# Second mixer: the attention half's output norm ahead of the S5 half's, and S5 tiles interleaved with attention units four to seven

## The chip, the cores and the metric

The kernel runs on one core of a Trainium2 chip. Five engines work side by side and meet only through semaphores: TensorE (PE in the profile; PEld is its weight load), VectorE (DVE), ScalarE (ACT), GpSimd (POOL) and SyncE (SP), which issues most of the transfers. The metric is the time of one execution in device microseconds, as the median of several runs. All times below are of that kind.

## What is computed

Two transformer blocks over 512 tokens of width 1024, in float32. The change lies in the second block's mixer. It projects the normed input to `u`, `q`, `k`, `v`; an S5 state-space layer runs on `u` (a linear recurrence over the tokens, then `gelu`, then a gate), and attention with a sliding window of 128 tokens and a sink runs on `q`, `k`, `v`. Each half gets its own RMS norm, and both together go through `w_out`:

```python
    _, _, s_re, s_im = lax.associative_scan(combine, (a_re_t, a_im_t, bu_re, bu_im), axis=1)
    y = (jnp.einsum("blgp,ghp->blgh", s_re, c_re) - jnp.einsum("blgp,ghp->blgh", s_im, c_im)
         + d_skip.reshape(N_SSM_GROUPS, SSM_GROUP) * ug)
    z = jax.nn.gelu(y.reshape(bsz, seq, D_SSM))
    y_ssm = z * jax.nn.sigmoid(z @ w_glu + b_glu)
...
    m = jnp.maximum(jnp.max(logits, axis=-1, keepdims=True), sink)
    p = jnp.exp(logits - m)
    probs = p / (jnp.sum(p, axis=-1, keepdims=True) + jnp.exp(sink - m))
    y_attn = jnp.einsum("bnhgqk,bnkhd->bnqhgd", probs, v_band)
...
    mixed = jnp.concatenate([_rms(y_ssm, out_norm_ssm), _rms(y_attn, out_norm_attn)], axis=-1)
    x = x + g1 * (mixed @ w_out)
```

After it comes the second block's feed-forward layer.

## The kernel before

Every engine has one hand-written list of instructions. No scheduler changes it: what stands first is issued first, and an instruction whose semaphore has not come holds all that is behind it on its engine. So the order of work in the second mixer is the order of the calls at the end of each engine's part.

**Number format.** A float32 product is made of three passes on PE: a tensor is split in `hi` (a rounded copy, made by ACT) and `lo` (the rest, made by DVE), and `hi*hi`, `hi*lo` and `lo*hi` are summed in a PSUM bank. Weights come in panels of 1 MB: SP loads a panel in `w_raw`, `split(n)` on ACT makes `w_hi`, `split(n)` on DVE makes `w_lo`. There are two buffers of each. The sums of squares, the transposes, scores and values work in plain float32.

**The eight PSUM banks** `B[0]` to `B[7]` are handed out by hand. Banks 0 to 3 are for attention units (even ones use 0 and 1, odd ones 2 and 3), bank 7 takes a unit's values, and the small functions `u2_bank`, `u_bank`, `input_bank`, `chunk_bank`, `turned_bank`, `glu_bank`, `out2_bank` say which bank a piece of S5 or of the output uses. Bank 5 takes the sum of squares of the S5 norm (`ps`), bank 7 that of the attention norm (`pa`).

**The attention** has eight units (four blocks of 128 queries, two key heads). One unit goes PE `sw_scores`, DVE `sw_max` (bias, row maximum), ACT `sw_exp` (four exponentials with their sums), DVE `sw_scale`, PE `sw_turn` (transposes), ACT `sw_turned` (copy to `pT`), PE `sw_values`, ACT `sw_out` (copy from bank 7 to `yat`). The next unit's `sw_values` waits for it, since bank 7 is the only one.

**S5** goes PE `project` (pieces of `u2_products`, 96 matmuls in all), ACT `u2_moved`, PE `chunk_turn`, ACT `u_moved`, PE `chunk_inputs`, DVE `chunks` (two halves, each a scan over 64 chunks), PE `within_chunks` and `from_states`, ACT `chunk_out`, PE `turn_back`, ACT `s5_gelu` (the gelu, then `z_hi`), DVE `z_split` (`z_lo`), PE `glu` (four tiles of 12 matmuls), ACT `gates`, DVE the product `ys`.

**The norms.** For `ps` and `pa` alike ACT makes four squares, PE sums them with four matmuls against `ones` (`norm`), ACT takes the inverse root (`norm_root`), DVE improves it in three steps, and then for each of four tiles DVE makes `h`, ACT `h_hi`, DVE `h_lo`. The squares of `ps` go through two slots of `tmp`, so the third and fourth wait for PE. Then PE multiplies with `w_out`: the first two panels tile by tile of the sum (`by_k`), S5 half (`ks` 0 to 3) first and the attention half after it, the last two panels as `features`. The norm `p2` and the feed-forward loops follow.

**ACT's function tables.** When ACT goes from one kind of function to another (exponential, gelu, sigmoid, inverse root), the compiler puts an `ACT_TABLE_LOAD` ahead.

SP's list waits for the last `project` matmul, then loads two tables for S5 and the first panels of `w_out`. The functions and lines that the steps below touch stand in the printed code.

Of the kernel before, what the change touches and what calls it, by code (L numbers as in the profile page):

```python
# [25 lines left out]
F32 = mybir.dt.float32  # L26
# [105 lines left out]
def build(nc, inp, rel_onehot, out):  # L132
# [12 lines left out]
    with ExitStack() as ctx:  # L145
# [53 lines left out]
        def overlay(size, *tiles):  # L199
# [55 lines left out]
         z_hi, z_lo, yat_sq) = overlay(  # L255
# [4 lines left out]
            (12, "wb", [P, NS, 2, 2, P // 2], F32), (16, "gate", [P, 4, T], F32),  # L260
# [4 lines left out]
            (12, "z_hi", [P, 4, T], F32R), (24, "z_lo", [P, 4, T], F32R), (4, "yat_sq", [P, 4, T], F32),  # L265
# [18 lines left out]
        def u_bank(q):  # L284

            return B[(5, 6, 4, 5)[q]]
# [5 lines left out]
        def chunk_bank(q):  # L292

            return B[(4, 7, 4, 7)[q]]

        def turned_bank(q):

            return B[(5, 6, 4, 5)[q]]

        def glu_bank(t):  # L300

            return B[(6, 4, 5, 6)[t]]

        def out2_bank(t):

            return B[(4, 6, 5, 0, 1, 2, 3, 4)[t]]
# [25 lines left out]
        NORM_PARTS = {"n1": (KD, KD), "nm": (KD, 2), "n2": (KD, 2), "p1": (KD, 2), "ps": (4, 4), "pa": (4, 4), "p2": (KD, 2)}  # L332
# [3 lines left out]
        for name in NORMS:  # L336
            before = [NORM_PARTS[b] for b in NORMS[:len(NORM)]]
            NORM[name] = sum(tiles for tiles, _ in before)
            NORM_SQ[name] = sum(NORM_PARTS[b][1] for b in NORMS[:len(NORM) - 1] if b != "pa")
# [304 lines left out]
        def _(act):  # L644
# [32 lines left out]
            def norm_cast(name, hi=h_hi, shift=None):  # L677

                for k in range(NORM_PARTS[name][0]):
# [348 lines left out]

            u2_moved(0)
            u2_moved(1)  # L1030
            sw_exp(0)
            u2_moved(2)
            sw_exp(1)
            sw_turned(0)
            sw_turned(1)
            sw_out(0)
            u2_moved(3)
            sw_out(1)
            u_moved(0)
            sw_exp(2)  # L1040
            for q in (1, 2, 3):
                u_moved(q)
            sw_exp(3)
            split(PART["glu"][0])
            sw_turned(2)
            sw_turned(3)
            sw_out(2)
            sw_out(3)
            chunk_out(0)
            chunk_out(1)  # L1050
            act.wait_ge(S("scan_out"), 4)
            s5_gelu((0, 1))
# [3 lines left out]
            sw_exp(4)  # L1056
            sw_exp(5)
            sw_turned(4)
            sw_turned(5)
            gates((0, 1))  # L1060
            sw_out(4)
            gates((2, 3))
            split(PART["glu"][0] + 1)
            sw_out(5)
            sw_exp(6)
            norm_squares("ps", ys, lambda eng, k: eng.wait_ge(S("glu_out"), k + 1))
            sw_exp(7)
            split(PART["glu"][0] + 2)
            norm_root("ps", T)
            sw_turned(6)  # L1070
            sw_turned(7)
            sw_out(6)
            sw_out(7)
            act.wait_ge(S("sw_out"), 2 * len(SW_UNITS))
            for k in range(4):
                act.activation(yat_sq[:, k, :], yat[:, k, :], ACT.Square).then_inc(S("yat_squared"), 1)
            norm_cast("ps", h_hi[:, 0:4])
            norm_root("pa", T)
            norm_cast("pa", h_hi[:, 4:8])
            n = PART["w_out2"][0]  # L1080
# [28 lines left out]
        def _(dve):  # L1109
# [15 lines left out]
            def norm(name, tiles, gain, shift=None, hi=None, lo=None, width=D, panel=None):  # L1125
# [9 lines left out]
                for k in range(count + 1):  # L1135
                    if k < count:
# [591 lines left out]
            chunks(0)  # L1728
            chunks(1)
            sw_max(4)  # L1730
            sw_max(5)
            split(PART["glu"][0])
            z_split(range(4))
            sw_scale(4)
            sw_scale(5)
            sw_max(6)
            sw_max(7)
            for t in range(4):
                dve.wait_ge(S("glu_gate"), t + 1)
                dve.tensor_tensor(ys[:, t, :], ys[:, t, :], gate[:, t, :], ALU.mult).then_inc(S("glu_out"), 1)  # L1740
            split(PART["glu"][0] + 1)
            sw_scale(6)
            sw_scale(7)
# [685 lines left out]
```

## Time and profile before

| | us |
|---|---|
| median of 3 runs | 1877.11 |
| lowest and highest | 1875.33, 1881.25 |
| the profiled execution's own time | 1880.06 |
| its span, first to last instruction | 1878.6 |
| PE busy | 1824.4 (97%) |
| DVE, ACT, POOL busy | 1027.0, 722.5, 168.9 |
| mean granted TensorE clock | 0.984 |

The span of the profiled execution is 1878.6 us, 1.5 less than its time; its time is 2.95 above the median. The profile counts from the first instruction. The second mixer's own stretch, from the first `project` matmul to the first matmul of the norm `p2`, is 1314.5 to 1490.2 us. A row of the timeline gives the start, the length, the engine, the line, and in brackets how long the engine had been idle before it and who ended that. Rows that follow each other without a gap are merged (x8 is eight instructions). A plain float32 matmul shows as two.

### The profile page before, as it was taken

The page shows a single profiled execution, that of the slowest core. Times are in us where ns is not written, and L with a number is a line of the kernel's source. Part 1 is how long each engine was busy: PE and PEld are TensorE (multiplying, and loading weights), DVE is VectorE, ACT ScalarE, POOL GpSimd, SP SyncE. Part 2 cuts the span into 40 slices and gives each one's busy share as a digit, 9 for nine tenths or more (in the row PEclk, how much of TensorE's full clock was granted, in tenths as well). Part 3 has the DMA queues.
Part 4 walks back from the last instruction along what each step waited for, and adds up shares of the span by engine and source line. Part 5 has one row for each costly group of instructions (what it writes and reads, how often), then busy time and mean ns, then how long its engine had stood idle before and what let it go on. Part 6 is the DMA issues. An engine that isn't in the chain of part 4 may idle for free.

```text
span 1878.6 us, 23478 instructions
## 1 busy us (share of the span) xinstructions
PE 1824.4 (97%) x8801; PEld 1450.6 (77%) x8801; DVE 1027.0 (55%) x1433; ACT 722.5 (38%) x1015; POOL 168.9 (9%) x232
## 2 busy tenths in 40 slices
PE   7999999999999999999999999998997999999998
PEld 5888888868887777876887788887974688888887
DVE  5655436464564556555788733436485455555433
ACT  4222222333434787422332222224545245555322
POOL 2222001110000000005111110100000300000000
PEclk9999999999999999999999999999998999999999
DMA  6766422233222112223654552234211223322222
GB/s 205 236 213 214 144 70 92 93 120 102 90 82 80 63 46 68 68 90 97 206 167 135 152 151 79 90 106 174 109 34 45 67 90 101 100 89 78 89 87 81
DMA packets 171691, 206.77 MB, mean 110 GB/s; under 512 B 18404, under 2 KB 150114, under 8 KB 171106
## 3 DMA queue, kind: packets, MB, share of 16 engines
q1 hardware_dynamic: 144994, 161.97, 26.4%
q0 software_dynamic: 12640, 38.55, 6.6%
q10 hardware_dynamic: 13984, 5.27, 1.2%
q8 instruction: 47, 0.77, 0.2%
q14 instruction: 26, 0.21, 0.0%
HBM read 190.29 MB, written 17.56 MB: 111 GB/s over the span
## 4 chain that ended last, share of the span: by engine, by line
PE 94%; DVE 3%; ACT 2%; issue 1%; DMA 0%; ACTq 0%; DVEq 0%
PE bank L1854 42%; PE bank L1818 35%; PE bank L2069 6%; PE bank L1786 2%; PE bank L1976 1%; PE bank L2093 1%; PE bank L2166 1%; PE bank L1833 1%; PE bank L1874 1%; PE bank L2104 0%; ACT prob L994 0%; PE bank L1905 0%; PE bank L2205 0%; PE bank L2095 0%; DVE scan_t L1657 0%
## 5 line engine op out<-in xcount | busy, mean ns | idle before, releaser
L659 ACT CAST w_hi<-w_raw 128x2048 fp32r<-128x2048 f32 x158 | 301.1, 1906 | 833.6 <-PE bank L1854 454.3
L1123 DVE TENSOR_TENSOR w_lo<-w_raw,w_hi 128x2048 fp32r<-128x2048 f32 x157 | 370.6, 2360 | 455.5 <-ACT w_hi L659 455.2
L1854 PE MATMUL bank<-h_hi,w_hi 128*128 128x512 f32 x1088 | 435.5, 400 | 13.4 <-ACT h_hi L683 8.9
L1854 PE MATMUL bank<-h_hi,w_lo 128*128 128x512 f32 x1088 | 433.2, 398 | 0.0
L1854 PE MATMUL bank<-h_lo,w_hi 128*128 128x512 f32 x1088 | 344.1, 398 | 0.0
L1854 PEld LDWEIGHTS bank<-h_hi,w_hi 128*128 128x128 f32 x1088 | 206.4, 190 | 65.9 <-issue 16.8
L1854 PEld LDWEIGHTS bank<-h_lo,w_hi 128*128 128x128 f32 x1088 | 206.0, 189 | 50.0
L1854 PEld LDWEIGHTS bank<-h_hi,w_lo 128*128 128x128 f32 x1088 | 206.4, 190 | 49.3 <-issue 0.2
L1818 PE MATMUL bank<-hid_hi,w_lo 128*128 128x512 f32 x528 | 208.8, 396 | 0.0
L1818 PE MATMUL bank<-hid_hi,w_hi 128*128 128x512 f32 x528 | 208.8, 396 | 0.0
L1818 PE MATMUL bank<-hid_lo,w_hi 128*128 128x512 f32 x528 | 208.8, 396 | 0.0
L1818 PEld LDWEIGHTS bank<-hid_hi,w_hi 128*128 128x128 f32 x528 | 99.2, 188 | 24.1
L1818 PEld LDWEIGHTS bank<-hid_lo,w_hi 128*128 128x128 f32 x528 | 99.2, 188 | 23.9
L1818 PEld LDWEIGHTS bank<-hid_hi,w_lo 128*128 128x128 f32 x528 | 99.2, 188 | 23.9
L589 POOL TENSOR_TENSOR tmp<-x 128x512 f32<-128x512 f32 x24 | 28.8, 1201 | 922.2 <-DVE x L1624 441.6
L1818 PE MATMUL bank<-w_hi,h_hi 128*128 128x512 f32 (+1 forms) x256 | 97.8, 382 | 0.0
L1818 PE MATMUL bank<-w_lo,h_hi 128*128 128x512 f32 (+1 forms) x256 | 97.4, 380 | 0.0
L1818 PE MATMUL bank<-w_hi,h_lo 128*128 128x512 f32 (+1 forms) x256 | 97.4, 380 | 0.0
L1272 DVE SCALAR_TENSOR_TENSOR mod_acc<-mod_raw,small,mod_acc 128x512 f32<-128x512 f32 x84 | 63.2, 752 | 28.7 <-DMA mod_raw<-in_w_mod 24.9
L1304 DVE TENSOR_TENSOR tmp<-tmp,bank 128x512 f32<-128x512 f32 x44 | 28.3, 684 | 91.7 <-PE bank L1854 91.7
L558 POOL DMA_DIRECT2D mod_raw<-in_w_mod x96 | 52.7, 549 | 191.3 <-DVE mod_acc L1269 147.4
L1766 DVE SCALAR_TENSOR_TENSOR tmp<-bank,vec,tmp 128x511 f32<-128x511 f32 x88 | 63.8, 746 | 6.5 <-DVE tmp L1766 1.7
(410 smaller groups left out, 2402.6 us busy)
## 6 DMA issues: line engine op xcount, KB each, us to landing
w_raw<-in_w_in SPq DMA_DIRECT2D x29, 1024.0 KB, 5.2
mod_raw<-in_w_mod POOLq DMA_DIRECT2D x96, 256.0 KB, 3.8
w_raw<-in_ffn_w_gate SPq DMA_DIRECT2D x22, 1024.0 KB, 7.0
w_raw<-in_ffn_w_up SPq DMA_DIRECT2D x22, 1024.0 KB, 5.5
w_raw<-in_w_up SPq DMA_DIRECT2D x22, 1024.0 KB, 5.1
w_raw<-in_ffn_w_down SPq DMA_DIRECT2D x16, 768.0 KB, 4.2
w_raw<-in_ffn_w_down SPq DMA_DIRECT2D x16, 640.0 KB, 3.9
w_raw<-in_w_out SPq DMA_DIRECT2D x8, 1024.0 KB, 5.0
```

What stands on the lines that cost most here:

```text
L558: pool.dma_start(mod_raw[:, k % MOD_SLOTS, :], wm[:, k, bass.ds(i * T + first * T, T)])\
L589: done(pool.tensor_tensor(tmp[:, min(k, 1), :], x[:, k, :], x[:, k, :], ALU.mult))
L659: act.copy(w_hi[i % 2][:], w_raw[i % 2][:]).then_inc(S("w_hi_done"), 1)
L1123: dve.tensor_tensor(w_lo[s][:], w_raw[s][:], w_hi[s][:].bitcast(F32), ALU.subtract).then_inc(S("w_split"), 1)
L1272: ins = dve.scalar_tensor_tensor(mod_acc[:], mod_raw[:, k % MOD_SLOTS, :], small[:, k:k + 1], mod_acc[:], ALU.mult, ALU.add)
L1304: dve.tensor_tensor(tmp[:, 2 + t, :], tmp[:, t, :], B[2 + t][:], ALU.mult).then_inc(S("hid"), 1)
L1766: dve.scalar_tensor_tensor(y[:, back:], up[:, :T - back], col_at(f"conv_w_2:{2 - back}", i * 2, KF * half + t), y[:, back:], ALU.mult, ALU ...
L1786: mm = pe.matmul(out_ap, stationary, moving, start=first and i == 0, stop=last and i == len(terms) - 1)
L1818: mm = pe.matmul(out_ap, stationary, moving, start=first and i == 0, stop=last and i == total - 1)
L1833: pe.matmul(sum_bank(name)[:], ones[:], square, start=direct == tiles and d == 0, stop=d == direct - 1).then_inc(S("norm_summed"), 1)
L1854: mm = pe.matmul(bank[:], w[:, k, at], h[:, k, :], start=k == first and part == 0 and i == 0, stop=k == last and part == 1)
L2069: mm = pe.matmul(beside_bank(name, t)[:], stationary, moving, start=j == 0, stop=j == 3 * k - 1)
```

## The change

Nothing is computed differently. It moves work and renames places.

- **Attention norm first.** `pa` is made before `ps` on ACT, DVE and PE. PE multiplies panel 0 with the attention half (`out2(0, "pa", ...)`), then sums the squares for `ps`, then panel 1 with the attention half, then panels 0 and 1 with the S5 half. `split(glu + 2)` on DVE comes between the two norms.
- **Squares of the S5 half** go to a tile of their own, `ys_sq`, made by ACT in one go behind `norm_cast("pa")`, and not through `tmp`.
- **Units and S5 pieces in another order.** On ACT the exponentials of unit zero stand ahead of the first `u2_moved`; units four and five run among `u_moved`, `chunk_out` and the gelu tiles; the exponentials of units six and seven stand ahead of the gates. On DVE units four and five are scaled between the two halves of `chunks`, and units six and seven ahead of the split of the first `w_out` panel. On PE `project` is cut 12, 24, 6, 26, 6, 6, 16 where it was 24, 12, 12, 30, 6, 6, 6; the scores of six and seven, and the values of four and five, stand ahead of the last `from_states`; two `glu` tiles stand ahead of the transposes of units six and seven, and the last one behind the values of both.
- **Banks and places** follow: the tables of banks, the waits at `chunk_turn`, `chunk_inputs`, `sw_values`, `within_chunks`, `turn_back`, and the overlay of the shared area (`scan_t`, `ys`, `gate`, `z_hi` move).

```diff
-            (0, "u2t", [P, NS, 2, TB, SG], F32), (0, "scan_t", [P, 4, NS // 2, NC], F32), (0, "ys", [P, 4, T], F32),
+            (0, "u2t", [P, NS, 2, TB, SG], F32), (12, "scan_t", [P, 4, NS // 2, NC], F32), (16, "ys", [P, 4, T], F32),
...
-            return B[(5, 6, 4, 5)[q]]
+            return B[(5, 6, 5, 5)[q]]
...
-            return B[(4, 6, 5, 0, 1, 2, 3, 4)[t]]
+            return B[(0, 1, 2, 3, 4, 6, 5, 0)[t]]
...
             norm_root("pa", T)
             norm_cast("pa", h_hi[:, 4:8])
+            for k in range(4):
+                act.wait_ge(S("glu_out"), k + 1)
+                act.activation(ys_sq[:, k, :], ys[:, k, :], ACT.Square).then_inc(S("ys_squared"), 1)
+            split(PART["glu"][0] + 2)
+            norm_root("ps", T)
+            norm_cast("ps", h_hi[:, 0:4])
...
-                if q == 3:
-                    pe.wait_ge(S("u_moved"), 1)
+                if q >= 2:
+                    pe.wait_ge(S("u_moved"), (1, 3)[q - 2])
...
-                pe.wait_ge(S("u_moved"), 3 + half)
+                pe.wait_ge(S("u_moved"), 2 + 2 * half)
...
                 if u == 4:
-                    pe.wait_ge(S("o_out"), 4)
+                    pe.wait_ge(S("o_out"), 2)
...
-            for part, ks in enumerate(((0, 1, 2, 3), (4, 5, 6, 7))):
-                for i in range(2):
-                    pe.wait_ge(S("w_split"), n + i + 1)
-                    by_k(n + i, [out2_bank(2 * i), out2_bank(2 * i + 1)], h_hi, h_lo,
-                         lambda k: pe.wait_ge(S("norm_split"), NORM["pa"] + k - 3 if k >= 4 else NORM["ps"] + k + 1), ks)
+
+            def out2(i, name, ks):
+
+                pe.wait_ge(S("w_split"), n + i + 1)
+                by_k(n + i, [out2_bank(2 * i), out2_bank(2 * i + 1)], h_hi, h_lo,
+                     lambda k: pe.wait_ge(S("norm_split"), NORM[name] + k % 4 + 1), ks, first=4, last=3)
+
+            out2(0, "pa", (4, 5, 6, 7))
+            norm("ps")
+            out2(1, "pa", (4, 5, 6, 7))
+            out2(0, "ps", (0, 1, 2, 3))
+            out2(1, "ps", (0, 1, 2, 3))
```

ACT of the kernel before, from the copies of units four and five (`pT`) over the gates to the two inverse roots:

```order
L1003 COPY pT<-bank 128x512 x4
L1027 ACT_TABLE_LOAD
L1027 ACTIVATE gate<-bank,vec 128x512 x2
L1011 COPY yat<-bank 64x2x128 x2
L1027 ACTIVATE gate<-bank,vec 128x512 x2
L659 CAST w_hi<-w_raw 128x2048
L1011 COPY yat<-bank 64x2x128 x2
L994 ACT_TABLE_LOAD
L994 ACTIVATE prob,stat<-prob,stat 128x256 x4
L995 ACTIVATE stat<-stat 128x4
L670 ACTIVATE tmp<-ys 128x512 x4
```

Ahead of the exponentials of unit six stand four gates, a panel split and unit five's copy; the squares of `ps` come next, and unit seven's exponentials behind them.

ACT of the changed kernel, from the last two gelu tiles (`ys`, `z_hi`) to the attention norm's squares:

```order
L1021 CAST z_hi<-ys 128x512 x2
L994 ACT_TABLE_LOAD
L994 ACTIVATE prob,stat<-prob,stat 128x256 x4
L995 ACTIVATE stat<-stat 128x4
L994 ACTIVATE prob,stat<-prob,stat 128x256 x4
L995 ACTIVATE stat<-stat 128x4
L1027 ACT_TABLE_LOAD
L1027 ACTIVATE gate<-bank,vec 128x512 x2
L1003 COPY pT<-bank 128x512 x4
L1027 ACTIVATE gate<-bank,vec 128x512
L1011 COPY yat<-bank 64x2x128 x4
L1027 ACTIVATE gate<-bank,vec 128x512
```

Both units' exponentials now stand right behind the gelu tiles and ahead of every gate, with no panel split among them.

PE of the kernel before, from the sum of squares of `ps` in bank 5 to the first matmul with `w_out`:

```order
L1833 MATMUL bank5<-tmp,ones 128x512 x4
L2244 MATMUL bank0<-ident,prob 128x128 x4
L2244 MATMUL bank1<-ident,prob 128x128 x4
L2244 MATMUL bank2<-ident,prob 128x128 x4
L2244 MATMUL bank3<-ident,prob 128x128 x4
L1786 MATMUL bank7<-pT,v2 128x512 x4
L1833 MATMUL bank7<-yat_sq,ones 128x512 x4
```

The sum of `ps` stands ahead of units six and seven, and their transposes and values ahead of the sum of `pa`.

PE of the changed kernel, the end of `out2(0, "pa")` and the start of `out2(1, "pa")`:

```order
L1869 MATMUL bank0<-h_lo,w_hi0 128x512
L1869 MATMUL bank1<-h_lo,w_hi0 128x512
L1848 MATMUL bank5<-ys_sq,ones 128x512 x4
L1869 MATMUL bank2<-h_hi,w_hi1 128x512
L1869 MATMUL bank2<-h_hi,w_lo1 128x512
```

The sum of `ps` now stands between 24 matmuls of panel 0 and 24 of panel 1. The sum of `pa` stands directly ahead of the first of these 48.

## Rows read from the trace of the kernel before

**Rows 1.** The page, part 1: busy time, share of the span, instructions.
```profile
PE 1824.4 (97%) x8801; PEld 1450.6 (77%) x8801; DVE 1027.0 (55%) x1433; ACT 722.5 (38%) x1015; POOL 168.9 (9%) x232
```
**Rows 2.** Waits of PE, 1318 to 1475: in total, times, longest.
```profile
PE bank L1833 <- ACT tmp L670: 5.5, 1, 5.5
PE bank L1818 <- DVE z_lo L1721: 3.7, 1, 3.7
PE bank L1786 <- ACT pT L1003: 2.0, 1, 2.0
PE bank L2244 <- DVE prob L1716: 1.7, 2, 1.0
PE bank L1833 <- ACT yat_sq L1076: 1.5, 1, 1.5
PE bank L1786 <- ACT yat L1011: 0.9, 1, 0.9
PE bank L2295 <- ACT oc L985: 0.5, 1, 0.5
```
**Rows 3.** Stretches of PE: length, busy, granted clock, DMA share, GB/s.
```profile
1392.70:1399.50 6.80, 5.04 (x12) 0.50 0.47 157
...
1420.00:1426.80 6.80, 5.41 (x7) 0.50 0.45 154
...
1433.70:1440.50 6.80, 5.75 (x7) 0.50 0.40 139
```
**Rows 4.** Timeline of PE: start, us, line, what.
```profile
1349.26 7.36 PE L2205 MATMUL bank<-ident,u2t 128*128 128x64 f32 x64
...
1394.46 0.77 PE L1818 MATMUL bank<-z_hi,w_hi 128*128 128x512 f32 x1 [3.67 <-DVE z_lo L1721]
...
1399.64 1.03 PE L2244 MATMUL bank<-ident,prob 128*128 128x128 f32 x8
...
1421.39 6.38 PE L1833 MATMUL bank<-tmp,ones 128*128 128x512 f32 x8 [5.51 <-ACT tmp L670]
1427.61 1.04 PE L2244 MATMUL bank<-ident,prob 128*128 128x128 f32 x8
...
1441.90 3.70 PE L1833 MATMUL bank<-yat_sq,ones 128*128 128x512 f32 x8 [1.51 <-ACT yat_sq L1076]
1445.04 0.79 PE L1854 MATMUL bank<-h_hi,w_hi 128*128 128x512 f32 x1
```
**Rows 5.** Timeline of ACT: last copy of `u2t`, last gate, table load, squares.
```profile
1348.56 0.65 ACT L974 COPY u2t<-bank 128x256 f32<-128x256 f32 x2 [3.46 <-PE bank L2166]
...
1414.21 0.69 ACT L1027 ACTIVATE gate<-bank,vec 128x512 f32<-128x512 f32 x1 [1.32 <-PE bank L1818]
...
1417.36 1.28 ACT L994 ACT_TABLE_LOAD   x1
...
1441.22 2.19 ACT L1076 ACTIVATE yat_sq<-yat 128x512 f32<-128x512 f32 x4
```
**Rows 6.** Timeline of DVE and ACT: panel split, last gelu tiles.
```profile
1389.66 2.29 DVE L1123 TENSOR_TENSOR w_lo<-w_raw,w_hi 128x2048 fp32r<-128x2048 f32 x1
...
1391.75 1.14 ACT L1021 CAST z_hi<-ys 128x512 fp32r<-128x512 f32 x2
1391.87 2.49 DVE L1721 TENSOR_TENSOR z_lo<-ys,z_hi 128x512 fp32r<-128x512 f32 x4
```
**Rows 7.** Timeline of ACT and DVE: the norm `pa`.
```profile
1447.25 0.69 ACT L675 ACTIVATE rstd<-bank,small 128x512 f32<-128x512 f32 x1
...
1451.59 0.69 DVE L1147 TENSOR_TENSOR h_lo<-tmp,h_hi 128x512 fp32r<-128x512 f32 x1
...
1452.86 0.69 DVE L1147 TENSOR_TENSOR h_lo<-tmp,h_hi 128x512 fp32r<-128x512 f32 x1
```
**Rows 8.** Stretches: length, PE, PEld, DVE, ACT, POOL busy, granted clock.
```profile
1390.00:1445.00 55.00, 40.35 (x155) 23.37 (x151) 28.16 (x42) 35.83 (x77) 0.00 (x0) 0.81 0.17 58
1445.00:1467.50 22.50, 22.50 (x97) 17.99 (x96) 14.59 (x19) 6.33 (x8) 4.31 (x3) 1.00 0.00 1
```

More of the change, by code:

```diff
@@ L338, in build @@
             NORM[name] = sum(tiles for tiles, _ in before)
-            NORM_SQ[name] = sum(NORM_PARTS[b][1] for b in NORMS[:len(NORM) - 1] if b != "pa")
+            NORM_SQ[name] = sum(NORM_PARTS[b][1] for b in NORMS[:len(NORM) - 1] if b not in ("pa", "ps"))
             NORM_SUM[name] = sum(direct + (direct < tiles) for tiles, direct in before)
@@ L1047, in _ @@
             sw_out(2)
+            sw_exp(4)
+            sw_exp(5)
+            u_moved(2)
             sw_out(3)
+            u_moved(3)
+            split(PART["glu"][0])
+            split(PART["glu"][0] + 1)
             chunk_out(0)
             chunk_out(1)
-            act.wait_ge(S("scan_out"), 4)
-            s5_gelu((0, 1))
+            sw_turned(4)
+            sw_turned(5)
+            s5_gelu((0, ))
+            sw_out(4)
+            s5_gelu((1, ))
+            sw_out(5)
             chunk_out(2)
@@ L1055, in _ @@
             s5_gelu((2, 3))
[L1056 to L1059, printed above, removed]
+            sw_exp(6)
+            sw_exp(7)
             gates((0, 1))
[L1061 to L1069, printed above, removed]
             sw_turned(6)
             sw_turned(7)
+            gates((2,))
             sw_out(6)
             sw_out(7)
+            gates((3,))
             act.wait_ge(S("sw_out"), 2 * len(SW_UNITS))
@@ L1123, in split, with norm @@
                 dve.tensor_tensor(w_lo[s][:], w_raw[s][:], w_hi[s][:].bitcast(F32), ALU.subtract).then_inc(S("w_split"), 1)
-            def norm(name, tiles, gain, shift=None, hi=None, lo=None, width=D, panel=None):
+            def norm(name, tiles, gain, shift=None, hi=None, lo=None, width=D, panel=None, between={}):
                 hi, lo = (h_hi, h_lo) if hi is None else (hi, lo)
@@ L1727, in _, with gated @@
                 sw_scale(u + 1)
[L1728 to L1729 removed]
             sw_max(4)
             sw_max(5)
+            chunks(0)
+            sw_scale(4)
+            sw_scale(5)
+            chunks(1)
+            sw_max(6)
+            sw_max(7)
             split(PART["glu"][0])
             z_split(range(4))
[L1734 to L1738, printed above, removed]
+            sw_scale(6)
+            sw_scale(7)
+            split(PART["glu"][0] + 1)
+            def gated(t):
                 dve.wait_ge(S("glu_gate"), t + 1)
                 dve.tensor_tensor(ys[:, t, :], ys[:, t, :], gate[:, t, :], ALU.mult).then_inc(S("glu_out"), 1)
[L1741 to L1743 removed]
+            for t in range(4):
+                gated(t)
+            norm("pa", yat, lambda k: col("out_norm_attn_2", k), hi=h_hi[:, 4:8], lo=h_lo[:, 4:8], width=T)
             split(PART["glu"][0] + 2)
             norm("ps", ys, lambda k: col("out_norm_ssm_2", k), hi=h_hi[:, 0:4], lo=h_lo[:, 0:4], width=T)
[L1746 removed]
             n, panels, _ = PART["w_out2"]
@@ L2325, in _ @@
             sw_scores(3)
-            project(6)
             sw_values(1)
-            for q in range(4):
-                chunk_turn(q)
-            chunk_inputs(0)
+            project(16)
+            chunk_turn(0)
+            chunk_turn(1)
             sw_turn(2)
@@ L2334, in _ @@
             sw_values(2)
+            sw_scores(5)
+            chunk_inputs(0)
+            chunk_turn(2)
+            sw_values(3)
+            chunk_turn(3)
+            within_chunks(0)
             chunk_inputs(1)
-            sw_scores(5)
-            sw_values(3)
-            within_chunks(0)
             within_chunks(1)
@@ L2341, in _ @@
             from_states(1)
+            sw_turn(4)
+            sw_turn(5)
             within_chunks(2)
```

77 lines of the change are left out of this document (39 added, 38 removed).

## The prediction

> **What bounds the kernel now.** I read the page first. PE is busy 97% of the span and no other engine more than 55% [rows 1], so time can only be won where PE stands still or runs slowly. The change leaves every matmul as it is; it decides what PE finds in front of it. So I went to PE's waits inside the second mixer, then to the granted clock of its stretches, then to the timelines of PE, ACT and DVE around each wait.
>
> The waits [rows 2] add up to 5.5 + 3.7 + 2.0 + 1.7 + 1.5 + 0.9 + 0.5 = 15.8 us. The reader should see who is named: the squares of the S5 norm, the split of the gelu tiles, the copies and probabilities of units six and seven, the squares of the attention norm.
>
> The clock is the second loss. Three times the granted clock is 0.50, that is 1.2 GHz and not 2.4, for 6.8 us, each time after or amid waits: it fell 1.9 us into the wait for `z_lo`, late in the wait for the first square of `ps`, and behind the short waits of units six and seven. In these stretches PE was busy for 5.04 + 5.41 + 5.75 = 16.2 us [rows 3]. At half the clock half of that is lost: 8.1 us. A second way to count agrees. The first `glu` tile took 1399.64 - 1394.46 = 5.2 us for 12 matmuls, 0.43 each, where 96 at the full clock fill the 22.5 us of the next stretch, 0.234 each [rows 4, 8]; and the four sums for `ps` took 1427.61 - 1421.39 = 6.2 us against 1445.04 - 1441.90 = 3.1 for `pa` [rows 4]. (That one holds short waits for squares beside the clock.)
>
> Together 15.8 + 8.1 = **23.9 us are lost** in the second mixer before, nearly all of it from 1390 to 1445. That is the pot from which the change can win.
>
> [...] In 1390 to 1445 PE is busy for 40.35 of 55 us, PEld for only 23.37, where a stretch without a gap has PEld at 17.99 of 22.50, or 80% [rows 8]. [...]
>
> **The change part by part.** I carried the new order forward: each engine takes its list in turn, each step starts when its engine is free and its semaphore has come, with the lengths of the rows. What PE still waits for is this.
>
> *Start, to the end of `project`.* The first exponentials no longer stand behind copies of `u2t`, and 26 matmuls cover them: the first wait for `prob` (0.7 of the 1.7 in [rows 2]) goes. But the last 16 `project` matmuls now stand directly ahead of `chunk_turn`, which needs their copy. Before, the values of unit one lay between and hid it: the copy starts at 1348.56 and PE goes on at 1349.26 [rows 4, 5]. Bare, it costs the length of those values, **1.0 us**.
>
> *Units four and five among the scans.* Here each wait has a cover, and I name the thin ones. `chunk_turn(3)` waits for the third `uc`, which ACT copies behind the exponentials of units four and five: 1.0 us to spare. `chunk_inputs(1)` waits for the fourth `uc`, behind unit three's copy: 0.9. `from_states(0)` waits for the first scan, behind four row maxima: 1.3. The values of unit five wait for bank 7: **0.2 us**. The second scan on DVE starts 4 us later, behind the scaling of units four and five, but `from_states(2)` stands later too and has 4 to spare. SP's list is the same and its table loads still follow `project`, with over 10 us to spare. The panel split on ACT ahead of `chunk_out(0)` falls in time in which ACT waits for PE anyway.
>
> *The wait for `z_lo`.* Before, DVE was busy with a panel split until 1391.87, so all four tiles of `z_lo` came at the end (2.49 us), though `z_hi` was ready earlier [rows 6]. Now two tiles are done long before, and the chain is ACT's alone: last `z_hi` at 1392.9, one `z_lo` of 0.7, so PE starts 0.7 us earlier. 3.7 becomes **3.0**; the 0.5 wait for `oc` goes, as the `turn_back` steps are spread out.
>
> *Units six and seven.* The 5.5 us wait was ACT's list: from the last gate at 1414.21 a panel split, unit five's copy, a table load at 1417.36, the exponentials, and only then a square [rows 5]. All of this now lies ahead of the gates, under 24 `glu` matmuls. So do the exponentials of unit seven (1.0 of `prob`) and the copies of `pT` that stood behind the S5 root (2.0). Gone: 5.5 + 1.0 + 2.0. Bank 7 still holds the values of unit seven back: **0.9**, as before.
>
> *The squares for `pa`.* PE ends `glu(3)`, ACT must make the last gate (0.69) and the first square (0.6 of 2.19 for four) before PE can sum [rows 5]; with the hand-overs **1.6 us**, where it was 1.5.
>
> *The chain of `pa` is now bare.* This is the price. Before, the sums for `pa` were followed by the S5 half of `w_out`. Now nothing stands between them and `out2(0, "pa")`. From the root to the first `h_lo` the chain took 1451.59 + 0.69 - 1447.25 = 5.03 us [rows 7]; with the end of the sums ahead and PE's start behind, **5.4 us**. No table load adds to it: it runs while PE sums.
>
> *The chain of `ps` is covered, barely.* The sums for `ps` follow `out2(0, "pa")`, and 24 matmuls of panel 1 stand behind: 24 x 0.234 = 5.6 us of cover for a chain of 5.3 to 5.4. After that DVE delivers a tile each 1452.86 - 1451.59 = 1.27 us [rows 7], and PE needs 6 x 0.234 = 1.4. I take nought, with 0 to 0.5 as bounds. The last two panels are as they were.
>
> *Idle after:* 1.0 + 0.2 + 3.0 + 0.9 + 1.6 + 5.4 = 12.1 us, against 15.8. **Gain 3.7.**
>
> *Clock after.* The trace of before doesn't show the new order's clock, so I go by its two like waits. A wait of 3.7 brought a spell of 6.8 us that began 1.9 us in; a wait of 5.5 brought one that began 4.1 us in, since PE stopped at about 1415.9 [rows 3, 4]. If the waits of 3.0 and 5.4 do the same, 6.8 - 1.1 = 5.7 and 6.8 - 1.3 = 5.5 us of work fall in them: 11.2 against 16.2, and half of the difference is **2.5 us gained**. The third spell had waits of 1.0 and 2.0 us ahead of it, and the new order has 0.9 and 1.6 there; I take it as gone. The bounds are one spell fewer (2.8 us more gained) and one more (3.4 less).
>
> The sum is 3.7 + 2.5 = 6.2 us. Against the profiled execution that makes 1880.06 - 6.2 = 1873.9; that execution is 2.95 above the median, and I put the gain on the median: 1877.11 - 6.2 = **1870.9 us**. What is uncertain in the hand-overs (some 0.1 us for each of a dozen) makes 1 us to either side.
>
> **The rivals.**
>
> *A third spell.* Waits of 0.9 and 1.6 us stay around the values of unit seven, with only `glu(3)` between, and before waits of 1.0 and 2.0 were enough. For it: they lie close. Against: they are shorter and hold 2.8 us of full work between them. Price: 6.8 us of work at half the clock, 3.4. Time: 1870.9 + 3.4 = 1874.3. This would be no change.
>
> *A thin cover tears.* If the S5 chain takes over 5.6 us, or the third `uc` is over 1.0 us late, PE waits for the rest, one to one, and what hangs on it moves too. For it: covers of 0.2 to 1.3 us at five places. Against: my rows include the hand-overs at most of them. Price 1 to 3: 1873 on the middle.
>
> *One spell less.* If the wait for `z_lo` is so short that the clock holds, 2.8 more are won: 1868.1. For it: the chain has the least in front of it of all. Against: 3.0 is not far from 3.7, and waits of 2.0 and less had a spell behind them.
>
> *Slower: the clock stays down.* From the first `glu` tile to the end of the 96 `w_out` matmuls PE has 45 us of work, broken by waits of 0.9, 1.6 and 5.4. If each recovery is cut off by the next wait, the half clock holds on. Each 6.8 us spell more costs 3.4, so two more eat the whole gain and from four more it is slower than 1882.7, the bound of what can be measured: 1870.9 + 4 x 3.4 = 1884.5. Against: before, the clock was back at 1.00 after each of three spells though the waits went on, and the 22.5 us behind them ran at 1.00 [rows 3, 8].
>
> *It doesn't do what it says.* The lists are fixed, so the order does change; but the waits could only move, the bare chain of `pa` (5.4) taking the place of the one removed (5.5). It gives 1877 if all other gains fail as well. Against: the waits of 2.0, 1.0, 0.7 and 0.5 go for reasons of their own.
>
> **How the numbers follow.** A difference of 0.3%, 5.6 us, is about what a measurement of this kernel can tell from none. The forecast, 1870.9 with a range of its own from 1869 to 1873, has 0.50. The third spell has 0.18, a torn cover 0.12, one spell less 0.10, nothing gained 0.05, slower 0.05. Faster by over 5.6 us means below 1871.5: three quarters of the forecast (0.38), one spell less (0.10) and a little of the torn covers (0.02), 0.50. Slower by over 5.6 us has 0.05. The rest, 0.45, is within 0.3%. The range of 8 in 10 runs from 1867 to 1876: below it lies half of the one-spell-less case, above it the slower one and nothing gained.
>
> **What would show it.** Right: PE has no wait for an S5 square and none for `pT`; one wait of 5.2 to 5.6 at the first `w_out` matmul; 2.6 to 3.3 ahead of `glu(0)`; 1.0 ahead of `chunk_turn(0)`; none at the first matmul of `out2(1, "pa")`; PE's waits in the mixer sum to 12; two stretches with the granted clock at 0.50, not three. Wrong: waits for `uc` or for the scans, a second wait of some us at panel 1, or a third stretch at 0.50 between `glu(0)` and `w_out`. The rest of the kernel, up to 1314 us and from the norm `p2` on, should take as long as before.

## The result, and the profile after

The changed kernel takes 1871.3 us in the median of 8 runs (1870.9 to 1875.5). The kernel before took 1880.4 in the median of 8 (1875.1 to 1881.3): the three runs shown ahead and five beside the changed kernel, four of which lie above 1880. The ratio is 0.9964, 95% interval 0.9953 to 0.9976: 0.36% faster, some 6.8 us. The medians lie 9.1 us apart and the means 6.9 (1879.0 and 1872.1), so the ratio is the safer figure. The same kernel run again with the experiments gave 0.9965 (0.9951 to 0.9978). The profiled execution took 1870.98 us, its span is 1869.5.

The page, part 1, of the changed kernel; it answers to [rows 1]:

```profile
PE 1819.3 (97%) x8801; PEld 1450.8 (78%) x8801; DVE 1026.7 (55%) x1433; ACT 721.8 (39%) x1014; POOL 168.9 (9%) x232
```

PE is busy 5.1 us less and the span is 9.1 shorter, so the share reads 97% as before. PE's waits in the second mixer, the view of [rows 2] (us in total, times, longest):

```profile
PE bank L1869 <- DVE h_lo L1153: 5.2, 1, 5.2
PE bank L1829 <- DVE z_lo L1727: 3.0, 1, 3.0
PE bank L1848 <- ACT yat_sq L1075: 1.3, 1, 1.3
PE bank L1797 <- ACT yat L1011: 0.9, 1, 0.9
PE bank L2220 <- ACT u2t L974: 0.7, 1, 0.7
```

Five waits, 11.1 us, where seven made 15.8. The S5 squares, the copies of `pT`, the probabilities and `oc` are no longer waited for. The two stretches at half clock, as [rows 3] shows three (columns: length, busy of PE, PEld, DVE, ACT, POOL, then granted clock, DMA share, GB/s):

```profile
1397.97:1404.80 6.83, 5.85 (x14) 4.62 (x15) 3.56 (x8) 6.78 (x21) 0.00 (x0) 0.50 0.22 75
1428.69:1435.52 6.83, 5.92 (x14) 4.75 (x15) 3.95 (x7) 5.39 (x9) 0.00 (x0) 0.50 0.01 2
```

Between them the clock is 1.00, that is 2.4 GHz. PE's timeline at the places that the prediction named, first and last row marking the mixer's stretch (it answers to [rows 4]):

```profile
1312.94 0.51 PE L2181 MATMUL bank<-w_hi,h_hi 128*128 128x512 f32 x1
...
1347.39 3.79 PE L2220 MATMUL bank<-ident,u2t 128*128 128x64 f32 x32 [0.74 <-ACT u2t L974]
...
1398.95 0.77 PE L1829 MATMUL bank<-z_hi,w_hi 128*128 128x512 f32 x1 [3.00 <-DVE z_lo L1727]
...
1429.60 0.77 PE L1869 MATMUL bank<-h_hi,w_hi 128*128 128x512 f32 x1 [5.21 <-DVE h_lo L1153]
1430.16 0.63 PE L1869 MATMUL bank<-h_hi,w_lo 128*128 128x512 f32 x1
1430.58 0.63 PE L1869 MATMUL bank<-h_hi,w_hi 128*128 128x512 f32 x1
...
1440.98 0.79 PE L1869 MATMUL bank<-h_hi,w_hi 128*128 128x512 f32 x1
...
1446.97 0.40 PE L1869 MATMUL bank<-h_hi,w_hi 128*128 128x512 f32 x1
...
1481.43 1.94 PE L1848 MATMUL bank<-tmp,ones 128*128 128x512 f32 x4
```

and DVE's first `h_lo` of `ps`:

```profile
1445.93 0.69 DVE L1153 TENSOR_TENSOR h_lo<-tmp,h_hi 128x512 fp32r<-128x512 f32 x1
```

The bare chain of `pa` is the wait of 5.21, and behind it matmuls stand 0.43 us apart, not 0.234. The chain of `ps` ends at 1446.62 and PE needs it at 1446.97: covered, with 0.35 us to spare. Both lengths were some 0.3 to 0.4 longer than forecast: from the first matmul of panel 1, at 1440.98, the cover is 5.99 us (forecast 5.6) and the chain 5.64 (5.3 to 5.4). The spare time came out right because the two errors cancel.

The mixer's stretch is taken here from the first `project` matmul to the last row above, in which PE sums squares for `p2`; the first matmul of `p2` stands 0.86 us ahead of that row in both kernels. It takes 1481.43 - 1312.94 = 168.49 us. In the kernel before it ended here:

```profile
1491.08 1.94 PE L1833 MATMUL bank<-tmp,ones 128*128 128x512 f32 x4
```

1491.08 - 1314.47 = 176.61, so the mixer gained 8.12 us. The code ahead of it is unchanged and was 1.53 us shorter in this execution: the two executions already differ by 0.8 us at 31 us from the start, and 0.6 more comes near 410 us, where a stretch at half clock lasted 3.4 us and not 6.8. Behind it 0.55 came back. 8.12 + 1.53 - 0.55 = 9.10, the whole difference of the spans, 1878.6 - 1869.5.

### The profile page after: what moved, and what is told of

Same layout as the page of the kernel before. It is cut to its first block, busy times and chain, and to the rows that moved or that the text cites. A ratio compares the mean times of both kernels' runs of the same rounds, so it can differ in the third digit from the quotient of the medians.

```text
span 1869.5 us, 23475 instructions
## 1 busy us (share of the span) xinstructions
PE 1819.3 (97%) x8801; PEld 1450.8 (78%) x8801; DVE 1026.7 (55%) x1433; ACT 721.8 (39%) x1014; POOL 168.9 (9%) x232
## 4 chain that ended last, share of the span: by engine, by line
PE 96%; ACT 2%; DVE 1%; issue 0%; DMA 0%; ACTq 0%; DVEq 0%
PE bank L1869 43%; PE bank L1829 35%; PE bank L2084 6%; PE bank L1797 2%; PE bank L1991 1%; PE bank L2181 1%; PE bank L2108 1%; PE bank L1848 1%; PE bank L1889 1%; PE bank L2119 0%; PE bank L1920 0%; PE bank L2236 0%; PE bank L2220 0%; PE bank L2287 0%; PE bank L2250 0%; PE bank L2298 0%
## 5 line engine op out<-in xcount | busy, mean ns | idle before, releaser
L1869 PEld LDWEIGHTS bank<-h_hi,w_hi 128*128 128x128 f32 x1088 | 207.1, 190 | 72.1 <-issue 22.8
L1829 PEld LDWEIGHTS bank<-hid_lo,w_hi 128*128 128x128 f32 x528 | 99.2, 188 | 23.9
```

The lines of the kernel that those rows point to most:

```text
L1829: mm = pe.matmul(out_ap, stationary, moving, start=first and i == 0, stop=last and i == total - 1)
L1869: mm = pe.matmul(bank[:], w[:, k, at], h[:, k, :], start=k == first and part == 0 and i == 0, stop=k == last and part == 1)
```

## The experiments

The theory: **the mixer's time is its dense work (what its matmuls take without a gap at the full clock), plus what PE waits, plus half of what it does at half clock, and nothing else.** The order of units and S5 pieces brings the gain; the norm swap costs. The chief rival: the norm swap is what pays. All ratios are against the kernel before, run on the same chip beside each.

### Which half of the change pays

The units as changed, the norms in the old order (PE's part; ACT and DVE follow it):

```diff
             sw_turn(7)
-            sw_values(6)
-            sw_values(7)
             glu(3)
-            norm("pa")
+            norm("ps")
+            sw_values(6)
+            sw_values(7)
+            norm("pa")
...
-            out2(0, "pa", (4, 5, 6, 7))
-            norm("ps")
-            out2(1, "pa", (4, 5, 6, 7))
             out2(0, "ps", (0, 1, 2, 3))
             out2(1, "ps", (0, 1, 2, 3))
+            out2(0, "pa", (4, 5, 6, 7))
+            out2(1, "pa", (4, 5, 6, 7))
```

> The changed order of units and S5 pieces stays, the order of the norms is that of before: glu(3) and the sums for ps stand ahead of the values of units six and seven, those values and the sums for pa cover the chain of ps, and 48 matmuls of the S5 half cover that of pa. Carried forward by hand with the rows' lengths, the waits left are 1.0 or less (u2t), 3.0 (z_lo), 1.7 (square of ps), 1.1 (bank 7), 1.9 (square of pa): about 8.5, and no bare norm chain. Theory (the gain came from the order of the units alone, and the norm swap cost its bare chain of 5.2 and a spell of the clock): 5.2 - 2.0 = 3.2 us of waits less and one spell less, 2.9: 1871.3 - 6.1 = 1865.2. Rival (the norm swap carries the gain): as slow as before, 1877 or more.

Measured: 1865.03 us, ratio 0.9930 (0.9916 to 0.9945). Its waits:

```profile
PE bank L1828 <- DVE z_lo L1726: 3.0, 1, 3.0
PE bank L1847 <- ACT yat_sq L1079: 1.5, 1, 1.5
PE bank L1847 <- ACT ys_sq L1072: 1.3, 1, 1.3
PE bank L1796 <- ACT yat L1011: 0.9, 1, 0.9
PE bank L2219 <- ACT u2t L974: 0.7, 1, 0.7
```

No `h_lo` among them, 7.4 us in all, and one stretch at half clock. The kernel before with the swap alone (the tail of the change on the front of before; ACT's part of it):

```diff
             sw_out(5)
             sw_exp(6)
-            norm_squares("ps", ys, lambda eng, k: eng.wait_ge(S("glu_out"), k + 1))
             sw_exp(7)
-            split(PART["glu"][0] + 2)
-            norm_root("ps", T)
...
-            norm_cast("ps", h_hi[:, 0:4])
             norm_root("pa", T)
             norm_cast("pa", h_hi[:, 4:8])
+            for k in range(4):
+                act.wait_ge(S("glu_out"), k + 1)
+                act.activation(ys_sq[:, k, :], ys[:, k, :], ACT.Square).then_inc(S("ys_squared"), 1)
+            split(PART["glu"][0] + 2)
+            norm_root("ps", T)
+            norm_cast("ps", h_hi[:, 0:4])
```

> The kernel before with the norm swap alone (pa first, squares of S5 in a tile of their own, w_out in the changed order); units and S5 pieces as before. Theory (the swap by itself costs): PE waits some 6.7 us for the scaled probabilities of unit six and seven where it waited 5.5 for the squares and did the sums of ps meanwhile, the waits for pT go (-2.0), and the bare chain of pa adds 5.4; carried forward by hand 4 us of waits more, and one or two spells of half clock more (3.4 each, cut by overlap). 1877 to 1880 + 4 + 3 = 1884 to 1887, slower than before by 0.3 to 0.5%. Rival (the swap pays by itself): at or below 1874.

Measured: 1881.44 us, ratio 1.0014 (1.0005 to 1.0023). PE's timeline at its two long waits:

```profile
1422.27 4.04 PE L2250 MATMUL bank<-ident,prob 128*128 128x128 f32 x16 [6.66 <-DVE prob L1718]
...
1441.83 0.76 PE L1860 MATMUL bank<-h_hi,w_hi 128*128 128x512 f32 x1 [5.22 <-DVE h_lo L1149]
```

The waits are as expected (6.7 and 5.2), the direction too, though the interval lies barely above 1. The size was not: I had expected 1884 to 1887, with 4 us more of waits and 3 us more of half clock. The profile has 3.3 more of waits, and three stretches at half clock, as before, of which one is 3.4 us long and not 6.8. The four kernels together:

| ratio to before | norm of S5 first | norm of attention first |
|---|---|---|
| units as before | 1 | 1.0014 |
| units as changed | 0.9930 | 0.9964 |

The intervals stand above. The rival falls. The reordering of the units is worth 13 us with the norms in the old order and 9.4 with them swapped; the norm swap costs 2.6 us on the old order of units and 6.4 on the new. Each of these is good to 2 to 4 us.

### Is the cover of the `ps` chain what hides it?

```diff
             out2(0, "pa", (4, 5, 6, 7))
-            norm("ps")
             out2(1, "pa", (4, 5, 6, 7))
+            norm("ps")
```

> One part of the change undone: the sums for ps stand behind panel 1's attention half and no longer ahead of it, so nothing covers the S5 norm's chain. Theory (waits and half clock make the time, and the 24 matmuls of panel 1 hide a chain of 5.3 us): a second bare wait of 5.2 to 5.4 us for the first h_lo of ps, and the clock falls once more around it for 3 or 7 us (1.5 to 3.4). 1871.3 + 5.3 + 1.5 to 3.4 = 1878 to 1880. Rival (DVE and ACT would have finished the chain anyway, the cover is not what hides it): no new wait, 1871 to 1872.

Measured: 1880.69 us, ratio 1.0007 (0.9998 to 1.0016): the whole gain of the change is gone. A wait and three stretches from its profile:

```profile
PE bank L1869 <- DVE h_lo L1153: 10.4, 2, 5.2
```

```profile
1350.92:1357.75 6.83, 6.83 (x34) 6.13 (x33) 0.96 (x1) 2.93 (x5) 0.00 (x0) 0.50 1.01 432
...
1432.84:1439.67 6.83, 5.95 (x14) 4.74 (x15) 3.92 (x7) 5.39 (x9) 0.00 (x0) 0.50 0.01 2
1456.73:1460.14 3.41, 3.22 (x8) 2.58 (x9) 3.26 (x6) 1.24 (x2) 0.00 (x0) 0.50 0.00 0
```

The chain, once bare, costs 5.2 us of wait, and the clock falls once more (1456.73), which takes 3.22 / 2 = 1.6: 6.8 together. Another new stretch was not expected: at 1350.92, behind the wait of 0.74 for `u2t`, in code that is the same as in the change. It takes 3.4 us of this profile and is not the cover's doing. By the ratios the difference to the change is 8.1 us, good to 3, which fits these 6.8 and would fit 10 as well.

### Does the clock fall because PE stands still?

Here work is added whose result nobody reads: five plain float32 matmuls in the wait for `h_lo`.

```diff
+            for _ in range(5):
+                pe.matmul(B[2][:], ones[:], yat_sq[:, 0, :], start=True, stop=True)
             out2(0, "pa", (4, 5, 6, 7))
```

> Work is added: five plain float32 matmuls of 512 columns between the sums for pa and the first w_out matmul, whose result nobody reads. At 0.85 us each they take 4.3 of the 5.2 us in which PE waits. Theory (the clock falls because PE stands still, and the spell at half clock behind the wait costs 5.9 / 2 = 2.9 us): the wait shrinks to about 0.9, the first h_lo comes no later, the spell at 1428.7 goes, and the kernel is faster by 2.9 us though it does more: 1871.3 - 2.9 = 1868.4. Rival A (the spell has another cause, such as its place in the program or the load of the chip): the spell stays, 1871.3, or 1872 with more work at half clock. Rival B (PE's reads slow ACT or DVE in the chain): the h_lo comes later, slower than 1872.

Measured: 1870.26 us, ratio 0.9955 (0.9941 to 0.9969). By the ratios that is 1.7 us less than the change, but the intervals overlap, so the times alone don't show a gain here. The trace does:

```profile
1424.96 4.46 PE L2394 MATMUL bank<-yat_sq,ones 128*128 128x512 f32 x10
1430.33 0.47 PE L1869 MATMUL bank<-h_hi,w_hi 128*128 128x512 f32 x1 [0.92 <-DVE h_lo L1153]
1430.64 0.39 PE L1869 MATMUL bank<-h_hi,w_lo 128*128 128x512 f32 x1
1430.87 0.40 PE L1869 MATMUL bank<-h_hi,w_hi 128*128 128x512 f32 x1
```

The `h_lo` comes as late as in the change, counted from the sums, and the `w_out` matmuls behind it stand 0.23 us apart at once. The mixer's stretch shrinks from 168.5 us (the same in both profiles of the changed kernel) to 165.8. So the spell (a stretch at half clock) hangs on PE's standing still, and it costs 2.7 us. The median moved less than the trace; three of the six runs lie at 1871.8 to 1872.4, with a mean granted clock of 0.986 where the others have 0.988 to 0.991. They had more half clock somewhere; where, no profile shows. Both long waits filled (three more such matmuls, on `x`, in the wait for `z_lo`):

> As the run with five idle matmuls in the wait for h_lo, with three more (plain float32, 512 columns, result read by nobody) in the 3.0 us wait for z_lo. Theory of the clock (it falls because PE stands still): both spells go, z_lo comes no earlier, so the whole gain is the clock's: 5.75 / 2 + 5.91 / 2 = 5.8 us, 1871.3 - 5.8 = 1865.5, and the profile shows no stretch at 0.50 between the first project matmul and w_out. Rival (spells come from the load or place): a spell stays in the mixer, 1868.5 or more.

Measured: 1866.79 us, ratio 0.9939 (0.9924 to 0.9953), with 6.9 us of needless work. Both spells at the long waits are gone, but my "no stretch at 0.50" was wrong:

```profile
1348.67:1355.50 6.83, 6.83 (x33) 6.24 (x33) 1.02 (x1) 2.93 (x5) 0.00 (x0) 0.50 1.00 427
```

The same place as at 1350.92 above, behind the 0.74 us for `u2t`. It costs 6.83 / 2 = 3.4 us, 4.6 times the wait itself.

### The short wait for `u2t`

Of eight profiles of kernels with this wait, the changed kernel's two included, four show the clock fall 2.7 us behind its end, four don't. Covering it, with the values of unit one:

```diff
-            sw_values(1)
             project(16)
+            sw_values(1)
```

> The changed kernel with the values of unit one put back between the last project matmul and chunk_turn (and ACT's copy of them behind the last u2t copy), so that the bare wait of 0.74 us is covered. Of the seven profiles of kernels that have that wait, four show the clock fall right after it for 6.8 us (from 1348.7 to 1350.9 on), three don't. Theory (that wait starts the spell in some executions, and this is the spread of the changed kernel from 1871 to 1875): the spell never shows, the slow end of the runs comes down by 3 us, and all runs lie within 2 us; fastest runs 1870.9 - 0.5 = 1870.4, median 1870.4 to 1870.8. Rival (the spread comes from stretches before the second mixer): the runs spread over 4 us as in the changed kernel, median 1871 or more.

> The changed kernel once more, unchanged, beside the two others on the same chip. Theory: two kinds of executions, with and without a spell at half clock at about 1350 us: runs near 1871 and near 1874.5, median 1871 to 1874. Rival (the first result holds one kind only, and its slower runs were chance): all within 1 us of 1871.

Measured beside each other on one chip: covered 1869.52 us (1868.3 to 1872.5), ratio 0.9954 (0.9941 to 0.9967); the change again 1872.44 (1869.3 to 1873.4), 0.9965 (0.9951 to 0.9978). The profile of the covered one has no stretch at half clock near 1350:

```profile
1398.17:1401.58 3.41, 2.81 (x7) 2.26 (x8) 0.67 (x3) 3.40 (x11) 0.00 (x0) 0.50 0.27 89
1425.48:1432.31 6.83, 4.27 (x10) 3.43 (x11) 5.58 (x9) 4.31 (x8) 0.00 (x0) 0.50 0.01 2
```

PE has a wait of 0.17 us for `prob` left near there, and the mixer's stretch is 166.02 us. But the runs still spread over 4.2 us, where I expected 2, and the two intervals overlap: that covering this wait pays is not shown by the times. The lengths above say why that was too neat: the spells at the long waits also differ from run to run, here 2.81 + 4.27 = 7.1 us of work in them, 11.8 in the change, behind the same waits. The wait for `u2t` is one source of the spread, not the only one; how much is its own the intervals don't tell. The changed kernel run again gave neither of the two pictures: its six runs spread over 4.1 us, so they are not all within 1 us of 1871, but they form no group at 1874.5 either. In both kernels the slow runs are those with the lower mean clock (covered: 0.986 in the run of 1872.5, 0.987 to 0.989 in the others), so the spread does follow the half clock, wherever it falls.

The profiles do hold a difference between the two kinds. All eight have a stretch at half clock that ends some 31 us ahead of the mixer, and the same matmuls without a gap from there to the wait. Here is that stretch in the changed kernel, where the clock stayed up, and in the run with the cover gone, where it fell:

```profile
1275.09:1281.92 6.83, 4.84 (x12) 3.81 (x13) 6.67 (x11) 3.55 (x5) 0.00 (x0) 0.50 0.97 393
...
1275.83:1282.65 6.82, 4.90 (x12) 3.86 (x13) 6.66 (x11) 3.55 (x5) 0.00 (x0) 0.50 0.98 394
```

From its end to the end of the wait for `u2t` it is 1347.39 - 1281.92 = 65.47 us in the first and 1348.20 - 1282.65 = 65.55 in the second. In the four profiles without the spell this distance is 65.45 to 65.47, in the four with it 65.55 to 65.61. So the two kinds are told apart by a difference of 0.1 us in where the wait lies after the last change of the clock. Eight profiles found afterwards are no proof of a cause, and no run moved the wait by 0.1 us to test it.

### Versions that beat both

The sums for `ps` in the wait for `pa`'s chain, with the squares behind the root of `pa`, where ACT waits anyway:

```diff
             norm_root("pa", T)
-            norm_cast("pa", h_hi[:, 4:8])
             for k in range(4):
                 act.wait_ge(S("glu_out"), k + 1)
                 act.activation(ys_sq[:, k, :], ys[:, k, :], ACT.Square).then_inc(S("ys_squared"), 1)
+            norm_cast("pa", h_hi[:, 4:8])
...
             norm("pa")
+            norm("ps")
```

> The changed kernel with one thing moved: ACT makes the squares of the S5 half straight behind the root of pa, where it waits for DVE anyway, and PE sums them ahead of out2(0, pa), inside the bare wait of 5.2 us. Theory: the root ends at 1425.1 and the first h_hi is due at 1428.1, so four squares of 0.55 fit; PE waits 1.3 to 1.6 for the first of them, sums for 3.4, and waits 0.2 to 0.4 for h_lo. The waits fall by 5.2 - 1.9 = 3.3 us, no wait is left that is long enough to bring the clock down there, 2.9 more: 1871.3 - 6.2 = 1865.1. Rival (the squares push the casts of pa back, or the clock falls anyway behind waits of 1.3 and 1.5): 1868 to 1870.

Measured: 1867.24 us, ratio 0.9933 (0.9915 to 0.9951). ACT's row and PE's:

```profile
1428.07 2.18 ACT L1079 ACTIVATE ys_sq<-ys 128x512 f32<-128x512 f32 x4
1431.17 1.28 ACT L683 CAST h_hi<-tmp 128x512 fp32r<-128x512 f32 x2 [0.92 <-DVE tmp L1145]
```

```profile
1428.74 3.70 PE L1848 MATMUL bank<-ys_sq,ones 128*128 128x512 f32 x8 [1.30 <-ACT ys_sq L1079]
```

The squares fit ahead of the cast, and the wait for `h_lo` fell to 0.2. The median lies 2 us above the expectation. The profile names two things that I had not counted, though not which of them the median holds: panel 1's `w_lo` now comes 0.8 late, since PE is there sooner, and this profile too has the spell behind the wait for `u2t`, at 1349.84.

The first two `glu` tiles by tiles of `z` (`k` outside, both banks inside, each `k` waiting for its own `z_lo`), and `glu(2)` ahead of `sw_turn(6)`:

> The changed kernel with the first two glu tiles multiplied tile by tile of z, so that PE starts at the first z_lo and not at the fourth, and glu(2) ahead of the transposes of unit six. Theory: the wait of 3.0 shrinks to at most 0.3, and the spell at half clock behind it goes (5.75 / 2 = 2.9 us); PE reaches units six and seven 5 us earlier and waits there for probabilities and their copy, 0.7 + 0.9. The bare chain of pa stays with its spell. 1871.3 - (3.0 - 1.9) - 2.9 = 1867.3. Rival (the new waits of units six and seven bring a spell of their own): 1869 to 1871.

Measured: 1867.13 us, ratio 0.9942 (0.9923 to 0.9961). The wait for `z_lo` and its spell are gone; a wait of 0.8 for `pT` came. This profile too has the spell behind the wait for `u2t`, at 1349.15.

Everything together: norms in the old order, `glu` by tiles of `z`, and more work moved into each remaining wait (PE's part, against the changed kernel with its norms put back; on ACT the squares of `pa` are made in two pairs, the first ahead of unit seven's copy, and the sums for `pa` go to bank 4).

```diff
-            sw_values(1)
             project(16)
+            sw_values(1)
...
-            glu(0)
-            glu(1)
-            sw_turn(6)
-            glu(2)
+            glu_pair()
+            glu(2)
+            sw_turn(6)
             sw_turn(7)
             glu(3)
+            sw_values(6)
             norm("ps")
-            sw_values(6)
             sw_values(7)
             norm("pa")
```

> A version against all waits: units ordered as in the change, norms as before (S5 first), glu by tiles of z, values of unit six ahead of the sums for ps, those of unit seven between the sums for ps and pa, the first two squares of pa ahead of unit seven's copy, values of unit one between project and chunk_turn. Carried forward by hand: waits of 0.2 to 0.8 us at five or six places, 2.5 in all (11.1 in the changed kernel), the first w_out matmul 0.8 late. Theory: 8.6 us of waits and both spells (5.8) go: 1871.3 - 14.4 = 1857, with 2 us to either side. Rival (the clock falls in any case once or twice in the mixer): 1860 to 1863. Rival (PE, moving earlier everywhere, runs into SP's panel loads or DVE's list): over 1863.

Measured: 1856.31 us, ratio 0.9880 (0.9862 to 0.9899). With the root of `ps` ahead of the first two squares of `pa`:

> The version against all waits with one repair: its first w_out matmul waited 0.80 us for h_lo because the root of ps stood behind two squares of pa and the table load; the two squares now stand behind the root. Theory: root 0.85 us earlier, the wait of 0.80 goes, the one for w_lo of panel 1 (0.80) stays: 1856.3 - 0.8 = 1855.5. Rival (the squares of pa come late now and PE waits for them, one to one): 1856.3 or more.

Measured: 1855.29 us, ratio 0.9874 (0.9858 to 0.9890). The wait of 0.80 for `h_lo` is gone and the stretch fell from 154.10 to 153.25, though the two ratios can't be told apart. It is the fastest of all: 1.3% under the kernel before, 0.9% under the change. PE's waits in the mixer, and the whole mixer at the full clock:

```profile
PE bank L1872 <- DVE w_lo L1130: 0.8, 1, 0.8
PE bank L2262 <- DVE prob L1725: 0.2, 1, 0.2
```

```profile
1314.00:1467.00 153.00, 152.02 (x1255) 123.41 (x1255) 99.88 (x178) 80.75 (x173) 18.68 (x11) 1.00 0.22 78
```

### The account over all profiles

"Stretch" is the mixer as measured above, "clock" half of PE's busy time in the windows at 0.50, "unread" the added matmuls. The waits are sums of the rounded values that the profile prints.

| kernel | stretch | waits | clock | unread | rest |
|---|---|---|---|---|---|
| before | 176.61 | 15.8 | 8.2 | | 152.7 |
| changed | 168.49 | 11.1 | 5.9 | | 151.5 |
| norms alone | 178.69 | 19.1 | 7.0 | | 152.6 |
| norms back, units changed | 162.15 | 7.4 | 2.9 | | 151.8 |
| cover gone | 179.14 | 16.5 | 11.0 | | 151.7 |
| wait for `h_lo` filled | 165.81 | 6.8 | 2.9 | 4.3 | 151.8 |
| both filled | 166.43 | 4.0 | 3.4 | 6.9 | 152.1 |
| `ps` sums in the wait | 166.71 | 8.2 | 6.3 | | 152.2 |
| `glu` by tiles | 166.24 | 8.9 | 5.1 | | 152.2 |
| `u2t` covered | 166.02 | 10.6 | 3.5 | | 151.9 |
| all covered | 154.10 | 1.8 | 0 | | 152.3 |
| all covered, repaired | 153.25 | 1.0 | 0 | | 152.3 |

The second profile of the changed kernel gives 168.50, 11.1 and 5.9, as the first. The stretch runs over 26 us, the rest stays within 1.2. The matmuls of the mixer take 152 us at the full clock, and what a version costs beyond that is its waits and its half clock. What makes the 1.2 us between the rest of before and of the changed kernel is open. Counted by kind of matmul from start to start, less waits and half clock, most of it lies in the values of the units (12.6 us against 11.9) and the transposes of their probabilities (6.8 against 6.3), the pieces whose neighbours changed most.

## Why the prediction was right

**The sum.** Forecast 1870.9, measured 1871.3. By the trace the mixer gained 8.1 where I had 6.2: waits 15.8 - 11.1 = 4.7 (forecast 3.7), clock 8.2 - 5.9 = 2.3 (forecast 2.5), and 1.1 without a name. By the ratio the gain is 6.8, so its size was right. That the time itself came within 0.4 us was in part luck: the forecast took the gain off a median of 1877.11, which with five more runs became 1880.44.

**The pot of 23.9 us was real.** The last version took out nearly all of it: 176.6 - 153.3 = 23.4. For the part from 1390 to 1445 us busy time shows a room of 55 - 40.35 = 14.65 us [rows 8]. That is the waits there; the half clock makes 8.2 more, 22.8 together, which the last version shows to be winnable.

The Trainium skill ("Perfetto Trace Analysis", section Identifying the Most-Contended Engine) says that the busy share of the matmuls does not measure well how close TensorE is to its roofline, and names the busy share of the weight loads, beside the share of peak FLOPs, in its place. Worked out that way from [rows 8], with the 80% of the stretch without a gap as the full share, the room is 55 - 23.37 / 0.80 = 26 us, as an estimate. 22.8 is nearer to that than to 15, so the trace sides with the weight loads, though they overstate the room by 3 us.

**Term by term.** `h_lo` bare 5.2 (forecast 5.4), `z_lo` 3.0 (3.0), bank 7 0.9 (0.9), squares of `pa` 1.3 (1.6), `u2t` 0.7 (1.0), unit five 0 (0.2). All waits that I called gone are gone. The sizes were good because each chain was taken whole from a row; three were 0.2 to 0.3 too long, perhaps since I added hand-overs that the rows already held; that was not tested.

**The `ps` cover** held with 0.35 us to spare, where I had counted 0.2 to 0.3; as shown above, that is two errors of 0.3 to 0.4 us which cancel. It is the most valuable cover of the change: without it a wait of 5.2 and 1.6 of half clock come back, and the ratio is 1.0007.

**The clock.** That the waits for `z_lo` and `h_lo` would bring spells like those of the two long waits before held: 5.85 + 5.92 = 11.8 us of work against 11.2. The third spell did not come between `glu(0)` and `w_out`, in no profile of the changed kernel.

**What failed** is the step "bare, it costs the length of those values, 1.0 us". The wait itself was 0.74, but I priced it with no clock behind it, and looked for a third spell only around the values of unit seven. In four of eight profiles the clock fell at this shortest wait and took 3.4 us. That the changed kernel's own two profiles don't show it was luck: in both the wait fell 0.1 us nearer to the last change of the clock than in the four that have the spell. Its slowest run (1875.5) has a mean clock of 0.984 against 0.987 in the profiled one, and a spell of 6.83 us lowers the mean by some 0.002, so that run had one or two spells more; where, was not profiled.

**What I didn't see** is that the two halves of the change work against each other. The prediction carried both to one sum, which came out right, and called the bare chain of `pa` the price. It didn't ask what the price bought. The old norm order would have had the values of units six and seven as a cover for the chain of `ps`, and 48 matmuls for that of `pa`: 6.4 us better.

## What to carry to other kernels

Take a change apart by its lists before pricing it as a whole: each part against each, four kernels, tells whether one pays for the other. For each chain that ends in a matmul, ask which independent matmuls stand between its start and its end, and keep a table of them; here sums of squares, values and other tiles' products were enough to cover every chain. Price a wait on TensorE with the half clock that may follow: the two long ones of the change cost 3.0 + 2.9 and 5.2 + 3.0 us.

## What the hardware showed

**Unread work made the kernel faster.** Eight needless matmuls (6.9 us) in two waits took the ratio from 0.9964 to 0.9939 (the intervals touch at 0.9953). The engine no longer stood still, and the half clock at both waits didn't come.

**Long waits always brought the half clock, short ones sometimes.** In the thirteen profiles the mixer has 18 waits of 3.0 us or more, and at each of them the granted clock falls to 0.50, during the wait or within 1.6 us of its end. Three versions have no such wait: in two of them the clock stays at 1.00 throughout, and the third (both filled) has only the spell behind `u2t`. Short waits gave both pictures: behind those of 1.0 and 2.0 us the kernel before had a spell (1433.7), while waits of 0.9 and 1.3 us had none of their own in any version.

**A wait of 0.74 us was followed by 6.8 us at 1.2 GHz in four of eight profiles.** Ahead of it PE had run without a gap and at 1.00 for 65 us, in those with the spell and in those without. The one thing found to differ is the distance from the last stretch at half clock to this wait, larger by 0.1 us in those with the spell. In the three profiles with the wait covered by the values of unit one, and in the two kernels with the units in the old order, the clock stayed at 1.00 there. That the wait brings the spell is likely by this count and not proved.
